# Pooling mixer: bias and scale as single rows spread by matmuls, weights scaled by columns, additions moved off the Pool engine

## The reference

```
h = rms_norm(x, norm_mix[0])
# 4 channel groups of 256, trailing windows 2, 4, 8, 16
pooled = stack((c - lagged) / cnt for each group) - hg
mixed  = einsum('bsgc,gcd->bsgd', pooled, w) + b
x = x + mixed.reshape(bsz, s, D_MODEL) * scale
```

## Time and profile before

| | us |
|---|---|
| median of three runs | 1255.61 (1253.95 to 1256.03) |
| the profiled execution | 1248.94 |
| its span, first to last instruction | 1247.1 |
| PE busy in the span | 1218.8 (98%) |
| DVE, ACT, POOL busy | 287.8, 200.9, 49.5 |

### The profile page before, as it was taken

The page is one execution under the profiler, slowest core; times in us unless marked ns, Lnnn a source line. Parts: engine busy times, 40 slices in busy tenths (PEclk is TensorE's granted clock), DMA queues, the critical chain, the costliest instruction groups (busy, mean ns, idle before and its releaser), DMA issues.

```text
span 1247.1 us, 28427 instructions
## 1 busy us (share of the span) xinstructions
PE 1218.8 (98%) x13473; PEld 668.8 (54%) x13473; DVE 287.8 (23%) x381; ACT 200.9 (16%) x279; POOL 49.5 (4%) x46
## 2 busy tenths in 40 slices
PE   7999999989999999999999999999999999999995
PEld 6888888879753353345336334533633443363353
DVE  4645454458551010110101011010101101000122
ACT  4543434355530000000000000000000000000001
POOL 3000000011000000000000000000000000000000
PEclk9999999999999999999999999999999999999999
DMA  9966556423479999999999999999999999999991
GB/s 345 390 232 201 173 199 194 143 62 119 140 291 390 393 414 419 410 408 417 419 405 413 418 410 408 418 419 405 414 419 408 408 418 418 406 410 412 414 360 44
DMA packets 101499, 423.53 MB, mean 340 GB/s; under 512 B 9089, under 2 KB 17970, under 8 KB 101378
## 3 DMA queue, kind: packets, MB, share of 16 engines
q1 hardware_dynamic: 94288, 410.59, 83.6%
q0 software_dynamic: 2272, 7.15, 1.6%
q10 hardware_dynamic: 4818, 3.93, 0.9%
HBM read 416.78 MB, written 4.85 MB: 338 GB/s over the span
## 4 chain that ended last, share of the span: by engine, by line
PE 97%; DVE 2%; ACT 1%; DMA 0%; issue 0%; ACTq 0%; DVEq 0%
PE psum L735 46%; PE psum L746 23%; PE psum L647 8%; PE psum L649 8%; PE psum L648 8%; PE psum L655 1%; PE psum L716 0%; DMA consts<-in_table 0%; PE psum L907 0%; DVE x_res L1498 0%; PE psum L826 0%; PE psum L930 0%; PE psum L663 0%; PE psum L917 0%; PE psum L1028 0%; PE psum L876 0%
## 5 line engine op out<-in xcount | busy, mean ns | idle before, releaser
L735 PE MATMUL psum<-up,xg 128*32 128x448 f32 x6144 | 579.0, 539 | 0.6 <-DVE xg L1722 0.6
L735 PEld LDWEIGHTS psum<-up,xg 128*32 128x32 f32 x6144 | 199.5, 110 | 375.8 <-issue 373.5
L746 PE MATMUL psum<-down,hid_t 128*32 128x256 f32 x5376 | 291.5, 379 | 0.0
L746 PEld LDWEIGHTS psum<-down,hid_t 128*32 128x32 f32 x5376 | 174.7, 110 | 117.9 <-issue 3.9
L1470 DVE TENSOR_TENSOR sil<-sil,psum 128x1344 f32<-128x1344 f32 x16 | 24.9, 1554 | 753.6 <-PE psum L735 753.6
L1346 DVE TENSOR_TENSOR low<-raw,high 128x2048 fp32r<-128x2048 f32 x50 | 114.5, 2291 | 79.8 <-ACT high L1065 79.6
L1065 ACT ACTIVATE high<-raw 128x2048 fp32r<-128x2048 f32 x51 | 97.9, 1920 | 83.3 <-PE psum L649 81.7
L647 PE MATMUL psum<-high,a_hi 128*128 128x512 f32 x224 | 87.3, 390 | 0.4 <-DVE a_lo L1383 0.4
L649 PE MATMUL psum<-low,a_hi 128*128 128x512 f32 x224 | 87.2, 389 | 0.0
L648 PE MATMUL psum<-high,a_lo 128*128 128x512 f32 x224 | 87.1, 389 | 0.0
L1145 ACT ACTIVATE sil<-psum 128x1344 f32<-128x1344 f32 x16 | 20.7, 1291 | 409.0 <-PE psum L735 409.0
(11 more groups left out here) (215 smaller groups left out, 571.4 us busy)
## 6 DMA issues: line engine op xcount, KB each, us to landing
up<-in_moe_w SPq DMA_DIRECT2D x256, 896.0 KB, 13.6
down<-in_moe_w SPq DMA_DIRECT2D x112, 1024.0 KB, 12.9
raw<-in_ffn_w SPq DMA_DIRECT2D x42, 1024.0 KB, 5.3
raw<-in_w_q SPq DMA_DIRECT2D x4, 1024.0 KB, 5.1
raw<-in_w_o SPq DMA_DIRECT2D x4, 1024.0 KB, 4.9
y_rows<-y_sb ACTq DMA_DIRECT2D x28, 96.0 KB, 8.9
x_res<-in_x SPq DMA_DIRECT2D x2, 512.0 KB, 4.8
raw<-in_pool_w SPq DMA_DIRECT2D x1, 1024.0 KB, 10.7
```

The costliest lines, as they stand in the source:

```text
L735: mm = pe.matmul(out3[g * BLK:(g + 1) * BLK, r, :], xg[:, k, r * BLK:(r + 1) * BLK], w[:, g], start=k == 0, stop=k == DT - 1)
L746: mm = pe.matmul(Y[g * BLK:(g + 1) * BLK, r, :], hid_t[:, c, r, b * BLK:(b + 1) * BLK], w[:, bb, g * GW:(g + 1) * GW], start=c == 0 and b ...
```

## The change

The two rows of bias and scale are no longer copied to 128 partitions by DMA: each is loaded as one row on one partition, by the ACT queue ahead of the constants, and both are gone from the SP queue. DVE forms bias times scale on the one partition. PE spreads both rows over the 128 partitions with four matmuls whose stationary operand is a row of ones (the contraction is over one partition): bias times scale to banks 4 and 5, the scale to banks 6 and 7. Of the twelve warming matmuls two stay ahead of these and four behind. DVE adds banks 4 and 5 to `x_res`, half a tile at a time, and multiplies the pooling weights in place by banks 6 and 7. The result of the mixing matmuls then only has to be added to `x_res`. POOL has neither the product nor the two additions; its split of the first dense unit stays.

```diff
-            sp.dma_start(pool_rows[:, 1, :], bc(pool_scale[0])).then_inc(pool_in, 16)
-            sp.dma_start(pool_rows[:, 0, :], bc(pool_b.rearrange("o g d -> (o g d)"))).then_inc(pool_in, 16)
...
-            pool.wait_ge(pool_in, 32)
-            pool.tensor_tensor(pool_bs[:], pool_rows[:, 0, :], pool_rows[:, 1, :], ALU.mult).then_inc(pool_step, 1)
-            pool.wait_ge(pool_step, 1)
-            pool.wait_ge(xn_ready, NT)
-            for t in range(NT):
-                pool.tensor_tensor(x_res[:, t, :], x_res[:, t, :], pool_bs[:], ALU.add).then_inc(pool_ready, 1)
...
-            keep_warm(0, 12)
+            keep_warm(0, 2)
+            one_row = consts[0:1, C_ONE:C_ONE + P]
+            for row in range(2):
+                pe.wait_ge(rows_made, row + 1)
+                for half in range(2):
+                    mm = pe.matmul(banks[OUT[row][half]][:], one_row, pool_rows[:, row, half * CW:(half + 1) * CW],
+                                   start=True, stop=True)
+                mm.then_inc(rows_spread, 1)
+            keep_warm(0, 4)
...
+                if d == 6:
+                    pe.wait_ge(gains_ready, 1)
...
-            pe.wait_ge(landed[U_POOLW], 16)
-            pe.wait_ge(gains_ready, 1)
+            pe.wait_ge(x_biased, 2 * NT)
...
+                        pe.wait_ge(w_scaled, g // 2 + 1)
...
+            act.dma_start(pool_rows[:, 0, :], pool_b.rearrange("o g d -> o (g d)")).then_inc(pool_in, 16)
+            act.dma_start(pool_rows[:, 1, :], pool_scale).then_inc(pool_in, 16)
...
+            dve.wait_ge(pool_in, 32)
+            dve.tensor_tensor(pool_rows[:, 0, :], pool_rows[:, 0, :], pool_rows[:, 1, :], ALU.mult).then_inc(rows_made, 2)
...
+            dve.wait_ge(rows_spread, 1)
+            dve.wait_ge(xn_ready, NT)
+            for t in range(NT):
+                for half in range(2):
+                    s = slice(half * CW, (half + 1) * CW)
+                    dve.tensor_tensor(x_res[:, t, s], x_res[:, t, s], banks[OUT[0][half]][:], ALU.add).then_inc(x_biased, 1)
+
+            def scale_weights(h):
+                w = raw[U_POOLW][:, h * 1024:(h + 1) * 1024].rearrange("p (g k f) -> p g k f", g=2, k=2)
+                scale = banks[OUT[1][h]].rearrange("p (g f) -> p g f", g=2).unsqueeze(2).to_broadcast([P, 2, 2, 256])
+                dve.wait_ge(rows_spread, 2)
+                dve.wait_ge(landed[U_POOLW], 16)
+                dve.tensor_tensor(w, w, scale, ALU.mult).then_inc(w_scaled, 1)
...
+                scale_weights(b // 2)
...
-                    mm = dve.tensor_tensor(xn[:, t, s], banks[OUT[t][half]][:], pool_rows[:, 1, s], ALU.mult)
-                step(mm)
-                dve.wait_ge(pool_ready, t + 1)
-                dve.tensor_tensor(x_res[:, t, :], x_res[:, t, :], xn[:, t, :], ALU.add).then_inc(x_ready, 1)
+                    mm = dve.tensor_tensor(x_res[:, t, s], x_res[:, t, s], banks[OUT[t][half]][:], ALU.add)
+                mm.then_inc(x_ready, 1)
```

More of the change, by code:

```diff
@@ L206, in trunk_program @@
         b_lo = at("b_lo", [P, 2, NT, CW], F32R, o_b + 8 * K)
-        pool_rows = at("pool_rows", [P, 2, D], F32, o_b)
-        pool_bs = at("pool_bs", [P, D], F32, o_b + 8 * K)
+        pool_rows = at("pool_rows", [1, 2, D], F32, o_b)
         kv_hi = b_hi[:].rearrange("p a b c -> p (a b c)").rearrange("p (d t) -> p d t", d=DT)
@@ L351, in trunk_program @@
         vec_turned, gains_ready = sem("vec_turned"), sem("gains_ready")
-        pool_ready, pooled, mixed = sem("pool_ready"), sem("pooled"), sem("mixed")
+        pooled, mixed = sem("pooled"), sem("mixed")
+        rows_made, rows_spread, x_biased, w_scaled = sem("rows_made"), sem("rows_spread"), sem("x_biased"), sem("w_scaled")
         pooled_even, pooled_odd = sem("pooled_even"), sem("pooled_odd")
@@ L815, in _ @@
                     pe.wait_ge(vec_in, 16 * 7)
-                    pe.transpose(banks[7][:, 0:NV], vec_rows[:, :], ident[0:NV, 0:NV]).then_inc(vec_turned, 1)
+                    pe.transpose(banks[3][:, 0:NV], vec_rows[:, :], ident[0:NV, 0:NV]).then_inc(vec_turned, 1)
             pe.wait_ge(pooled, DT // 2)
-            pe.wait_ge(landed[U_POOLW], 16)
-            pe.wait_ge(gains_ready, 1)
+            pe.wait_ge(x_biased, 2 * NT)
             w = raw3(U_POOLW, 8)
@@ L1480, in _ @@
                 normalise(0, t)
+            dve.wait_ge(rows_spread, 1)
[10 more added lines that the diff above has]
+                dve.tensor_tensor(w, w, scale, ALU.mult).then_inc(w_scaled, 1)
             dve.wait_ge(vec_turned, 1)
-            dve.tensor_copy(gains[:], banks[7][:, 0:NV]).then_inc(gains_ready, 1)
+            dve.tensor_copy(gains[:], banks[3][:, 0:NV]).then_inc(gains_ready, 1)
             dve.wait_ge(gains_ready, 1)
@@ L1489, in _ @@
                 mm.then_inc(pooled_even, 1)
-            dve.wait_ge(pool_in, 32)
+                scale_weights(b // 2)
             for t in range(NT):
```

## The result

The changed kernel took **1261.95 us** (median of 7, 1260.72 to 1267.11), the kernel before 1255.61 (7 runs): **ratio 1.0065, interval 1.0051 to 1.0079**. It is slower. The medians alone are 6.3 us apart, a ratio of 1.0050, and the means of all seven 7.9 us (1263.4 and 1255.5): three of the changed kernel's executions took 1265 to 1267 us. 1255.2 was forecast, with a range up to 1259.3.

A forecast was written before the change was run, and what follows sets the result against it. PE was taken to bound the kernel, so moving the first dense matmul moves the end. 1.8 us lost before the bands and 2.2 gained behind the mixing gave 1255.61 - 0.4 = 1255.2 us, range 1252.2 to 1259.3.

The forecast's parts named there:

- The sum of -0.4 us: Whole kernel: 1.8 us lost on the way to the bands, 2.2 gained behind the mixing, 0.4 us less.
- the warming matmuls: Opening on PE: six remain of twelve, at 0.395 us each, 2.4 us, less 0.2 overlap where the bands begin.
- the bands: PE's matmuls ahead of mixing: begin at 11.5 us in place of 9.70, with mixing 5.96 us behind their start.
- I take 5.9, since the packets of one queue follow its issues: Constants, third in the ACT queue: two issues ahead cost 0.8 us, so they land at 5.9 in place of 5.12.
- I take 0.85, the nearest row: Four row matmuls ahead of the bands: 0.85 us each, 3.4 for four; bounds 0.43 and 1.7 each.
- the row matmuls run at the lower clock: Rival, opening on PE: four take 6.8 us, total 1258.6, up to +6 if the bands are caught; chance 0.16.
- L1498's loss: DVE's addition for tile 0 behind the mixing: stood until POOL's split was through, which cost 2.9 us.
- the scaling of the weights: DVE's multiplying of the pooling weights ahead of mixing: 1.22 us for 1024 columns, second product hidden by 1 us.
- the rows' landing and DVE's product: Opening: second row in at about 5.5 us, product ends at 6.7, xn at 9.8 at most, covered by PE.
- the 24.5 us given for additions held up by POOL: DVE's new additions: if POOL did block them, the first pair ends near 24.5 us, still ahead of the second mixing half.
- The gain behind the mixing: From mixing to the dense part: 5.1 us in place of 7.31, 2.2 gained.
- with slack in it: The 7.31 us from the end of mixing to the dense part, including PE's 2.14 us wait for DVE's first addition.

The follow-up runs named there:

- consts_late: The kernel before, with two unused 4 KB rows loaded by the ACT queue ahead of the constants: ratio 1.0024.
- consts_first: The changed kernel with the constants issued ahead of the two rows on the ACT queue: 1264.97 us, ratio 1.0083.
- full_rows: The changed kernel with the four row matmuls fed from all 128 partitions by identity or ones, same shape: 1257.48 us, ratio 1.0018.
- warm_first: The changed kernel with the constants issued first, ten warming matmuls ahead of the row matmuls and none behind: ratio 1.0065.
- zero_rows: The changed kernel, constants first, ten warming matmuls ahead, row matmuls contracting over 128 partitions, 127 holding zeros: ratio 1.0015 to the kernel before.
- before_again: The kernel before, unchanged, profiled a second time: 1257.49 us.
- psum_product: The kernel before, with DVE's product written back to PSUM and added in two halves, one operand in SBUF: ratio 0.9993.
- halves: The kernel before, product back to PSUM, mixing handed over by halves of a tile, five warming matmuls between tiles dropped: 1251.40 us, ratio 0.9973.

## Why the prediction was wrong

The frame held: PE bounds the kernel, what moves the first dense matmul moves the end, and the rest of the kernel did not react. The sum of -0.4 us failed in two terms. Set against the first profile, as the prediction was, the dense part starts at 36.77 where 29.7 was forecast, 7.1 us later: the constants 2.8, the row matmuls 3.7, the warming matmuls 0.8 (3.0 us for six at the lower clock, 2.2 forecast with the overlap), the bands 0.7, and behind the mixing 1.0 less than forecast.

- **The constants: 0.8 us forecast, 3.6 measured.** The step "I take 5.9, since the packets of one queue follow its issues" took the issue times for the whole cost. consts_late shows the 3.6 us by themselves, and consts_first that the order alone takes them away. By the DMA's list for the first 9 us the constants took 7.1 us from issue to landing, where the earlier trace rows has 4.3, so the issue itself came 0.8 us later (1.6 against 0.8): that part was right. The 2.8 us on top were put at nothing. Of them 1.6 lie between the issue and the first packet, which comes behind the two rows (packets of q10, above), and 1.1 between the first packet and the landing; why the rows hold the transfer up by more than their issue stays open.
- **The row matmuls and the clock: 3.4 us forecast, 7.1 measured, and the low clock lasted into the bands.** The step "I take 0.85, the nearest row" rested on the clock being up from the first matmul. It came from the 1.00 in the earlier trace rows, which says nothing ahead of the first change on record, and from a warming matmul of 0.395 us, which I took for one at full clock. Its weight loads of 0.331 us say that it was not; at 2.4 GHz five of them take 1.28 us, as behind the mixing of the changed kernel, where 0.39 to each made the forecast some 0.8 us too long. I had the right rival on paper, "the row matmuls run at the lower clock", put its cost at 3 to 6 us, and gave it 0.16 on the ground of that same column; its far end, 1261.6, lay outside the range, which ended at 1259.3. full_rows, warm_first and zero_rows show it, and go beyond it: the clock is low at the start of every one of these kernels, and what PE is given bears on how long it stays so, and on whether it falls again. The Trainium skill (TensorE: Matmul & The Clock Gate, "The HAM clock gate"), which I set against the trace, has the default right: cold until activity releases it. By it the first matmuls of both kernels are cold, as their weight loads are.

By ratios: late constants 0.0024 (3.0 us), and the one partition 0.0047 (1.0065 less 1.0018 of full_rows, 5.9 us; 4.5 us by the medians). What is left for the rest of the change is -0.0006, which intervals of 0.001 and more on each of the three ratios can't tell from nothing. By the dense starts, one execution each, the constants are 3.1 us (consts_late less before_again), the one partition 3.5 (changed less full_rows), and 0.9 is left of the 7.6, as much as zero_rows loses.

What was right: L1498's loss was POOL's split, and additions with a PSUM operand don't meet it (1.28 us under it in psum_product); the scaling of the weights takes 1.21 us (1.22 forecast) and is hidden; the rows' landing and DVE's product cost nothing in the changed kernel, since 4.46 + 1.21 is far ahead of PE, and xn is ready at 8.49 us, earlier than before and not later; PE waits for no DMA but the constants, so 1 MB less buys it nothing. Two readings were loose without harm. The new product of the two rows does have both operands in SBUF, but POOL had no work beside it. And the 24.5 us given for additions held up by POOL don't agree with the prediction's own 24.8 for the end of the split; nothing was held up. The gain behind the mixing was sized at 2.2 us; it is 3.2 against the first profile and 1.6 against the second. In before_again and consts_late PE idled 1.2 us there and not 2.14, and the clock of the earlier trace rows did not fall; so half of the stretch "with slack in it" was not there in them.

## What to carry to other kernels

Spreading a row by a matmul is cheap in instructions and was dear in clock here: the contraction over one partition kept PE busy while its clock fell to 1.2 GHz, and what runs behind it pays (in warm_first the bands took 11.2 us in place of 6.0). Where it is wanted, pad the contraction with zeros to 128 partitions. Judge the clock of a stretch by the duration of equal weight loads, not by the clock column, until the first change is on record. What PE's first matmul waits for is issued first in its queue, even ahead of 4 KB. And before a pile of work is moved to get two engines apart, try the smallest edit that takes one operand out of SBUF: it ended the hold-up in psum_product, though only halves, with the hand-over changed as well, was faster clear of noise.

## What the runs showed of the hardware

- A float32 matmul over one partition, 512 columns: 1.78 us each at the low clock (7.12 for four, from 9.87 to 16.99 in the changed kernel), 1.04 each in warm_first (4.17 for four), where the clock fell under the last of them. Over 128 partitions, of which 127 are zero: 0.89 (3.54 for four, zero_rows), and the clock stays up.
- The clock, once down, is not raised by every stream of matmuls: in warm_first and consts_first the bands, three matmuls of 128, 16 and 128 columns to a block, ran for 10 to 11 us at the lower clock with PE busy throughout. In the seven profiles that open with ten or twelve identity matmuls it rose 3.1 us (zero_rows) to 5.5 us (psum_product) behind the first one.
- Two loads of 4 KB ahead of one of 256 KB in the same queue move its landing from 5.1 to 8.7 us (consts_late), and its first packet from 2.4 to 4.9 us (changed kernel).
- An addition of 1024 columns on DVE with both operands in SBUF took 1.23 us alone, and 4.10, 3.22 and 3.16 us when POOL's split ran (both profiles of before, consts_late), ending 1.1 us behind the split; with one operand in PSUM, in two halves, 1.28 us under the split (psum_product, the changed kernel).
- The kernel before has two paces among the experts, 108.4 us for each or 109.5 to 109.9 for most, and medians of 1247.68 and 1254.9 to 1255.6 us in different batches. Their cause is open.
